# Weight slots behind the router, and when the fifth expert is loaded, in a four-layer diffusion trunk with mixture of experts

## The reference

```python
for i in range(DEPTH):
    sh1, sc1, g1, sh2, sc2, g2 = adaln(cond, w_mod[i], b_mod[i])
    h = modulate(x, norm_mix[i], sh1, sc1)
    x = x + g1 * mixer[i % 3](h)
    h = modulate(x, norm_ffn[i], sh2, sc2)
    x = x + g2 * moe(h, w_router, router_bias, w_gate[i], w_up[i], w_down[i])

def moe(h, ...):          # top 2 experts of the best of 4 groups
    a, u = h @ w_gate[e], h @ w_up[e]        # 1024 -> 256, every expert e
    return sum_e (silu(a) * u * gates[e]) @ w_down[e]
```

## Time and profile before

| | |
|---|---|
| time, median of 3 runs (lowest to highest) | 1669.51 us (1668.85 to 1675.49) |
| profiled execution: time / span | 1670.27 us / 1668.1 us |
| mean granted PE clock | 0.944 |
| PE busy | 1457.2 us, 87% of the span |
| DVE / ACT / POOL busy | 545.3 / 371.9 / 195.9 us |
| DMA | 428.68 MB, mean 257 GB/s |
| chain that ended last | PE 73%, DMA 9%, DVE 7%, issue 3%, ACT 3% |

### The profile page before, as it was taken

One profiled execution on the slowest core, in us unless ns is written; L12 is line 12 of the kernel. 1 busy time (PEld: TensorE's weight loads), 2 busy tenths in 40 slices (PEclk: granted clock), 3 DMA queues, 4 the chain that ended last, 5 costly groups with the idle time before them and its releaser, 6 DMA issues.

```text
span 1668.1 us, 26431 instructions
## 1 busy us (share of the span) xinstructions
PE 1457.2 (87%) x10704; PEld 859.9 (52%) x10704; DVE 545.3 (33%) x1329; ACT 371.9 (22%) x985; POOL 195.9 (12%) x286
## 2 busy tenths in 40 slices
PE   3999998988997997997987999989979999969973
PEld 1876774333775774332563456743326766843321
DVE  0137442212456423211522343232115256242104
ACT  1106321110214421111210343211112045211100
POOL 0100111101121021001100000210011000210011
PEclk9999998998998998999899999989999999979987
DMA  9899148999778137999758303479999871248981
GB/s 333 301 318 329 77 163 336 382 412 351 261 283 243 77 127 280 362 421 351 270 196 255 83 26 121 157 281 372 421 350 331 284 265 53 99 176 342 422 318 51
DMA packets 125027, 428.68 MB, mean 257 GB/s; under 512 B 13099, under 2 KB 55038, under 8 KB 100326
## 3 DMA queue, kind: packets, MB, share of 16 engines
q1 hardware_dynamic: 96854, 350.32, 55.6%
q0 software_dynamic: 21104, 72.71, 12.8%
q10 hardware_dynamic: 6944, 3.91, 0.8%
HBM read 389.20 MB, written 40.26 MB: 257 GB/s over the span
## 4 chain that ended last, share of the span: by engine, by line
PE 73%; DMA 9%; DVE 7%; issue 3%; ACT 3%; POOL 1%; ACTq 1%; SPq 0%; DVEq 0%; POOLq 0%
PE bank L1790 65%; DMA work<-in_moe_w_gate 3%; PE bank L1960 3%; DMA ring<-in_w_mod 2%; ACT pp L1133 2%; PE bank L2124 2%; DMA ring<-in_moe_w_gate 1%; DMA ring<-in_moe_w_down 1%; ACTq L662 1%; PE bank L1847 1%; POOL small L808 1%; DVE xn L1280 1%; PE bank L2008 1%; DMA ring<-in_mla_wukv 1%; DVE hT L1267 1%
## 5 line engine op out<-in xcount | busy, mean ns | idle before, releaser
L1790 PE MATMUL bank<-ring,pp 128*32 128x512 f32 x2320 | 357.2, 630 | 48.2 <-DMA ring<-in_moe_w_down 23.4
L1790 PE MATMUL bank<-ring,hT 128*128 128x256 f32 (+3 forms) x998 | 237.2, 397 | 14.4 <-DMA ring<-in_mla_wukv 10.1
L1790 PEld LDWEIGHTS bank<-ring,hT 128*128 128x128 f32 x998 | 183.5, 194 | 64.8 <-issue 28.7
L1790 PEld LDWEIGHTS bank<-ring,pp 128*32 128x32 f32 x2320 | 99.0, 115 | 213.8 <-issue 212.4
L1790 PE MATMUL bank<-work,pp 128*32 128x512 f32 x768 | 168.9, 608 | 0.0
L1790 PE MATMUL bank<-ring,xn 128*128 128x256 f32 x768 | 168.2, 380 | 0.0
L1790 PEld LDWEIGHTS bank<-ring,xn 128*128 128x128 f32 x768 | 145.0, 190 | 19.4
L1680 DVE TENSOR_TENSOR pp<-bank,pp 128x256 f32<-128x256 f32 x40 | 17.0, 425 | 337.3 <-ACT pp L1210 337.3
L1790 PE MATMUL bank<-V,pp 128*32 128x512 f32 x512 | 96.7, 614 | 10.8 <-issue 10.8
L1790 PE MATMUL bank<-ring,condT 128*32 128x256 f32 x1216 | 85.8, 425 | 17.5 <-DMA ring<-in_w_mod 17.5
L1133 ACT ACTIVATE pp<-bank,neg_max 128x384 f32<-128x384 f32 x192 | 96.6, 524 | 13.0 <-DVE neg_max L1573 10.1
(11 more groups left out here) (264 smaller groups left out, 1735.8 us busy)
## 6 DMA issues: line engine op xcount, KB each, us to landing
ring<-in_w_mod SPq DMA_DIRECT2D x76, 1024.0 KB, 8.8
ring<-in_moe_w_gate SPq DMA_DIRECT2D x40, 1024.0 KB, 11.0
ring<-in_moe_w_up SPq DMA_DIRECT2D x40, 1024.0 KB, 13.3
ring<-in_moe_w_down SPq DMA_DIRECT2D x37, 1024.0 KB, 9.5
hT<-h_slots POOLq DMA_DIRECT2D x36, 512.0 KB, 12.0
work<-in_moe_w_down SPq DMA_DIRECT2D x16, 1024.0 KB, 6.3
y_slots<-kT POOLq DMA_DIRECT2D x32, 512.0 KB, 9.0
gbc<-in_w_mod SPq DMA_DIRECT2D x14, 1024.0 KB, 9.1
```

Source lines behind the costliest of these rows:

```text
L1790: return pe.matmul(out, lhsT, rhs, start=start, stop=stop)
```

## The change

Four things. Of the eight modulation units behind the router, the four with v 0 may have slots 0 to 3, where now all eight have slots 4 to 7; the same line lets both `ukv` units have slots 0 to 3, where now they have 2 and 3. Planned times: the second four directly behind the routing products, the experts 3 us earlier, the mark `held` 2 us earlier, the mark `rows` gone, and experts from the fifth on open at `held`. The planned load of such an expert takes 2.9 instead of 2.8 us. In the program itself one wait is removed: SP waited for the read of block 1 (`g_in[1]`) ahead of the first held expert, besides `held_ready`.

```diff
-LOAD_SPAN, LOAD_SPAN_MOE, AHEAD = 2.45, 2.8, 16
+LOAD_SPAN, LOAD_SPAN_MOE, AHEAD = 2.45, 2.9, 16
@@ unit_times
-        run_mods(mods["route"][4:], at + 7.0)
-        mark["held", L], mark["rows", L] = now + 70.0, now + 82.0
-        now += 76.0
+        run_mods(mods["route"][4:], at + 3.0)
+        mark["held", L] = now + 68.0
+        now += 73.0
@@ homes
-    if name == "wo" or phase == "route":
+    if name == "wo" or phase == "route" and key[2] == 1:
         return [(slot,) for slot in (4, 5, 6, 7)]
-    if name == "ukv":
-        return [(2,), (3,)]
+    if name == "ukv" or phase == "route":
+        return [(slot,) for slot in (0, 1, 2, 3)]
@@ plan_ring, opens
         if name[:3] == "moe" and key[2] >= FIXED:
-            return mark["rows", phase[0]]
+            return mark["held", phase[0]]
@@ block.sync, fill_expert
                 if (L, FIXED) not in held_at and e >= FIXED:
                     sp.wait_ge(held_ready, L + 1)
-                    sp.wait_ge(g_in[1], 16 * (BLOCKS // 2 * L + 1))
                     held_at[L, FIXED] = None
```

## The result

The changed kernel takes 1698.31 us (median of 4 runs, 1693.0 to 1708.01), against 1671.78 us before (median of 4 runs on the same chips, 1668.85 to 1675.49). The ratio is 1.0164, with a 95% interval of 1.0112 to 1.0216. It is slower, as forecast, but by 27 us instead of 15, and the time lies above the range. The profiled execution has a span of 1695.4 us, 27.3 more than before.

A forecast was written before the change was run, and what follows sets the result against it. The prediction took the kernel for a TensorE chain with holes, block 1 released by PE's work and by its rows. Terms 20 + 5 + 2 - 12 = +15 us on 1670.27 gave 1685 us, range 1663 to 1695 held at 0.8.

The forecast's parts named there:

- nothing is given back later: After block 1: the earlier fifth expert only lengthens a dry spell of the queues; block 8's wait of 19.5 us moves unchanged.
- mla_wukv's wait: Layer 2: the second unit gets slot 0 and is in before 909.1, so the second value products end 12 us sooner.
- queues take turns by packet: Scatter (q0) beside weights in 8 KB rows (q1): a packet each in turn, so the scatter gets a third of the bytes.
- The slow block after the wait: Block after a long PE wait runs at a lower clock: 1.7 us more, three times, 5 us in the sum.
- The terms from S to block 1: S is the layer's first scatter; block 1 was to start later behind it: 20 us over layers 0 to 2, layer 3 2.
- I take 6.7, near the upper end.: Block 1's delay in each of layers 0 to 2, between ends of -0.9 and about +8 to +9; 20 us together.
- lands some tenths behind: Layer 0: at 280 the scatter has sent 3.08 of 3.15 MB and lands tenths later; rows at 285, block 1 8.0 late.
- upper bound all of them ahead of it, 2.1 / 0.412 = 5 us: Layer 3: expert 4's 2.1 MB delay the scatter at most 5 us; 4.8 taken, block 1 2 us later.
- Half late: Rival, chance 0.20: the scatter gets half of the bytes, block 1 is 4 us late; +6, 1676 us.
- rows in time: Rival, chance 0.12: the scatter is as early as now, no long wait, mla_wukv saves 12; 1655 us.
- full gain: Rival, chance 0.05: rows land 7 us earlier, so PE's 7.2 us in three layers and mla_wukv's 12 come through; 1636 us.
- the moved mla wait: Rival, chance 0.13: mla_wukv's wait only moves to vector work or another unit, so the 12 us are not saved; 1697 us.

The follow-up runs named there:

- run 6: Changed kernel with the units of experts 2 to 5 loaded in two halves each, rows of 4 KB instead of 8 KB: 1688.56 us, ratio 1.0119.
- run 5: Changed kernel with SP's wait for the read of block 1 put ahead of the sixth expert only: 1683.21 us, ratio 1.0074.
- run 8: Changed kernel with a hold ahead of expert 2's down weights: until block 1 is read, 1659.02 us; second form, until the scatter has landed, 1667.89 us.
- run 3: Kernel before with only the slots of the two mla_wukv units widened to 0 to 3: 1658.26 us, ratio 0.9927.
- run 4: Kernel before with only the first four modulation units behind the router moved to slots 0 to 3, wait kept: 1673.11 us, ratio 1.0032.

## Why the prediction was right in kind and too small

**Right.** That block 1's rows take the place of the modulation weights in the chain, in layers 0 to 2; that nothing is given back later; that mla_wukv's wait goes and no other comes; that queues take turns by packet (two thirds to one third with 8 KB against 4 KB rows, equal with 4 KB, shown by run 6). Block 0 was forecast at 262.0 and came at 263.0. The slow block after the wait was put at 1.7 us in three layers; it was 1.3, 0.9 and 1.8, and 1.5 in layer 3, which the sum left out: 5.4 in all, against 5.

**Terms of the sum that were mis-sized.** The terms from S to block 1 were 20 us for three layers and 2 for layer 3. They measured 28.7 and 8.0, so 8.7 and 6.0 too small. The mla_wukv stretch gave 3 back, which leaves the 12 us missed.

*"I take 6.7, near the upper end."* It was 9.5 to 9.6, above the end itself. Two steps failed. The first is the discount from 8.0 to 6.7 for a late sixth expert, which had no ground: it was issued at 270.35, as worked out. Without it the three layers come to about 25 (8.0, 8.9 and the middle). The second is "lands some tenths behind": by 280 us q0 had sent 3.09 MB of the scatter, where 3.08 was forecast, but the last 0.06 MB took 2.4 us more, to the landing at 282.45 (260.08 + 22.37 in the chain). So reads went at 282.74 where 281 was forecast, and rows came at 286.3 where 285. And 0.5 us came from the turn, which took 1.97 us after 16 us of waiting, against 1.09.

*Layer 3, "upper bound all of them ahead of it, 2.1 / 0.412 = 5 us".* This step failed too, for the other 6 us. The reads went out 7.5 us later, and landed in 6.5 us instead of 3.6 (layer 3, chain):

```profile
...
1499.37 12.12 DMA h_slots<-xn,row_of
...
1511.77 6.49 DMA hT<-h_slots
...
```

Three things are wrong. First, the rate: in 1498 to 1508 us the two queues moved 0.358 MB/us, not 0.412 (before, the scatter alone moved 0.367 in 1478.2 to 1486.2), and at this rate 2.1 MB take 5.9 us. Second, the bound treats 16 DMA engines as one pipe. The scatter has landed when the last of them has, and in 1509 to 1511 us of the changed kernel, shortly before the reads are issued at 1511.77, the queues are nearly idle and yet not through (the page's line of busy tenths, then of GB/s, in 40 slices of 0.05 us):

```profile
...
DMA  0020010010010010001001001001001099001081
GB/s 0 0 82 0 0 82 0 0 82 0 0 82 0 0 82 0 0 0 82 0 0 82 0 0 82 0 0 82 0 0 82 0 655 410 0 0 82 0 328 82
...
DMA packets 30, 0.12 MB, mean 59 GB/s; under 512 B 9, under 2 KB 9, under 8 KB 22
...
```

One packet at a time for 1.6 us: I read this as one engine that is behind while the others are done; no run shows the engines apart. A tail is there in the kernel before too, only shorter: in the last 2 us ahead of the landing q0 sent 117 packets in layer 3, here 12. By that the tail has about 1 us of the 7.5 (an estimate: 0.37 MB less at 0.358 MB/us); why an engine would fall behind is open. Third, I let the sixth expert meet the reads in no sum of layer 3, though it is issued at block 0's end there too; run 5 puts it at 2.7 us. It was first, 2.1 us ahead of the reads, as in run 8 (SP's timeline, then the queues in 1512 to 1516 us):

```profile
...
1509.66 0.33 SPq L673 DMA_DIRECT2D ring<-in_moe_w_gate  x1
...
```

```profile
...
q1 hardware_dynamic: 209, 1.58, 95.4%
q0 software_dynamic: 10, 0.04, 2.5%
...
```

**mla_wukv** was put at 12 us. Run 3 measures 12. The stretch in the trace of the changed kernel is 15.2 shorter, and 15.8 in that of run 3, where nothing ahead of layer 2 is changed. The other 3 lie in the last blocks of layer 1, in a wait that comes and goes between kernels with the same order there.

**The rivals.** Half late, rows in time and full gain are out by the reads' 28.5 to 29.8 us; the moved mla wait by run 3. The range stopped at 1695, since it took the bound of 5 us for layer 3 as sure and the upper end of the three layers as unlikely.

## What to carry to other kernels

A wait that keeps an engine's loads back may be what gives another queue its room: before taking it out, list which small transfers the critical path needs next and what will be queued beside and ahead of them. Of two things that release the same block, moving one forward gains nothing until the other moves too: the modulation units alone gained nothing (run 4), and with the scatter freed as well block 1 came 20.5 to 22.7 us behind the scatter in layers 0 to 2 instead of 25.5 to 27.4 (kernel before). The scatter freed alone, with the modulation units where they were, was not run. And "these bytes at the full rate" is not an upper bound: here the scatter and the weights beside it moved at 0.358 MB/us, not at the 0.412 seen elsewhere, and the last 0.06 MB of a scatter took 2.4 us.

## What the runs showed of the hardware that I had not expected

- Order of issue counts: a read of 0.5 MB issued 0.27 us behind a first MB of weights and 0.1 us ahead of a second took 8.9 us, and none of its packets moved for 4 us; issued 0.74 us ahead of the weights, it lost nothing, and its first packets moved after 1.1 us.
- 1.05 MB of weights beside a scatter of 3.15 MB delayed its landing by 4.4 us, 2.1 MB by 7.4 us, where the bytes alone would be 2.5 and 5.1 us at 0.412 MB/us.
- While both queues send, the size of a row settles how they share the engines: 388 packets against 388 gave 2.82 and 1.41 MB, and 458 against 461 gave 1.66 and 1.69 MB. It is not so in every stretch: in 1501 to 1503 us of the changed kernel q1 sent 86 packets and q0 26.
- Two kernels that differ only in a wait that is already met had medians of 1649.24 and 1659.02 us.
